# Moving the first mixer's causal convolution from VectorE to GpSimd

## The reference, cut to what matters

```
proj = x @ w_in                       # xm, zm, us: 512 channels each
xc = silu(causal_dwconv(xm, conv_w, conv_b))   # 4 taps per channel, plus bias
q, k = block-diagonal maps of xc;  v = block-diagonal map of xm
h = mlstm_chunkwise(q, k, v, gates of [q, k, v])
out_m = (headnorm(h) + skip * xc) * silu(zm)
y = gelu(s5_ssm(us, ...))             # a diagonal complex state space, 32 groups of 64 states
out_s = y * sigmoid(y @ w_glu + b_glu)
return concat(out_m, out_s) @ w_out
```

## Time and profile before

| | |
|---|---|
| time, median of 3 runs | 2026.87 us (2026.23 to 2027.75) |
| the profiled execution's own time | 2031.62 us |
| its span, first to last instruction | 2029.8 us |
| busy: PE, DVE, ACT, POOL | 1661.1, 736.8, 258.5, 94.4 us |
| mean granted clock of TensorE | 0.915 of full speed |
| the mixer's stage | about 1263 to 1375 us of the span |

### The profile page before, as it was taken

One profiled execution on the slowest core, in us unless ns is written; L12 is line 12 of the kernel. 1 busy time (PEld: TensorE's weight loads), 2 busy tenths in 40 slices (PEclk: granted clock), 3 DMA queues, 4 the chain that ended last, 5 costly groups with the idle time before them and its releaser, 6 DMA issues.

```text
span 2029.8 us, 25027 instructions
## 1 busy us (share of the span) xinstructions
PE 1661.1 (82%) x10024; PEld 996.5 (49%) x10025; DVE 736.8 (36%) x1491; ACT 258.5 (13%) x630; POOL 94.4 (5%) x125
## 2 busy tenths in 40 slices
PE   5999988866666578886757567989999999999998
PEld 3755553322222146332222124776997486769963
DVE  2764462211011127221101013974566323444672
ACT  1002120000000012000000002232111122311100
POOL 1001001000000000840000000000000000000000
PEclk9989999988787779998787888999999999999999
DMA  9989269999999995999999998204445273304351
GB/s 362 402 318 414 94 276 410 420 422 422 422 422 422 404 422 219 400 405 421 422 422 422 422 420 330 101 1 176 149 142 207 80 283 120 129 11 166 125 208 41
DMA packets 122677, 581.28 MB, mean 286 GB/s; under 512 B 10820, under 2 KB 15272, under 8 KB 67160
## 3 DMA queue, kind: packets, MB, share of 16 engines
q1 hardware_dynamic: 120416, 573.92, 70.6%
q0 software_dynamic: 1104, 2.86, 0.4%
q10 hardware_dynamic: 1064, 3.17, 0.4%
HBM read 578.88 MB, written 1.05 MB: 286 GB/s over the span
## 4 chain that ended last, share of the span: by engine, by line
PE 43%; DMA 33%; DVE 8%; PEld 8%; issue 4%; ACT 2%; SPq 1%; PEldq 1%; DVEq 0%; ACTq 0%
DMA ring_buffer<-in_exp_w 30%; PE ps L1472 7%; PE ps L2197 6%; PE ps L2168 6%; PEld ps L2168 5%; PE ps L1497 4%; PE ps L2886 4%; PE ps L1997 3%; DMA ring_buffer<-in_attn_w_in 1%; PE ps L997 1%; PE ps L2877 1%; SPq L1361 1%; PE ps L2139 1%; PEld ps L829 1%; DVE xn L537 1%
## 5 line engine op out<-in xcount | busy, mean ns | idle before, releaser
L1472 PE MATMUL ps<-ring_buffer,arena 128*32 128x512 f32 x1984 | 298.4, 760 | 174.6 <-DMA ring_buffer<-in_exp_w 171.7
L1472 PEld LDWEIGHTS ps<-ring_buffer,arena 128*32 128x32 f32 x1984 | 78.2, 135 | 381.1 <-issue 324.6
L1497 PE MATMUL ps<-ring_buffer,arena 128*32 128x512 f32 x1088 | 149.7, 701 | 87.3 <-DMA ring_buffer<-in_exp_w 75.4
L1668 DVE TENSOR_TENSOR arena<-arena,ps 128x512 f32<-128x512 f32 x18 | 19.2, 1064 | 412.5 <-PE ps L1472 412.5
L2168 PE MATMUL ps<-arena,ring_buffer 128*128 128x128 f32 x1152 | 133.9, 276 | 3.7 <-issue 3.7
L2168 PEld LDWEIGHTS ps<-arena,ring_buffer 128*128 128x128 f32 x1152 | 130.8, 192 | 5.7 <-issue 5.7
L1497 PEld LDWEIGHTS ps<-ring_buffer,arena 128*32 128x32 f32 x1088 | 40.1, 126 | 186.1 <-issue 145.5
L2197 PE MATMUL ps<-ring_buffer,arena 128*128 128x512 f32 x252 | 111.0, 594 | 3.4 <-issue 2.4
L2168 PE MATMUL ps<-hT,ring_buffer 128*128 128x128 f32 x864 | 99.4, 275 | 0.0
L2168 PEld LDWEIGHTS ps<-hT,ring_buffer 128*128 128x128 f32 x864 | 97.9, 192 | 0.0
L1686 DVE TENSOR_TENSOR arena<-ps,gates 128x512 f32<-128x512 f32 x16 | 11.1, 693 | 195.1 <-PE ps L1497 195.1
(11 more groups left out here) (570 smaller groups left out, 2096.6 us busy)
## 6 DMA issues: line engine op xcount, KB each, us to landing
ring_buffer<-in_exp_w SPq DMA_DIRECT2D x376, 1024.0 KB, 18.6
ring_buffer<-in_ffn_w SPq DMA_DIRECT2D x30, 2048.0 KB, 11.8
ring_buffer<-in_ada_w SPq DMA_DIRECT2D x24, 2048.0 KB, 17.5
ring_buffer<-in_c_w_in SPq DMA_DIRECT2D x8, 2048.0 KB, 13.0
ring_buffer<-in_attn_w_in SPq DMA_DIRECT2D x6, 2048.0 KB, 16.8
arena<-in_exp_w SPq DMA_DIRECT2D x6, 1024.0 KB, 8.1
ring_buffer<-in_ab_w_in SPq DMA_DIRECT2D x3, 2048.0 KB, 14.0
ring_buffer<-in_ffn_w SPq DMA_DIRECT2D x6, 1024.0 KB, 6.0
```

The costliest lines, as they stand in the source:

```text
L1472: ins = pe.matmul(ps[c, bank, :], tokens[:, 4 * phase + k, c], halves[j][:, k, :], start=(phase == 0 and k == 0), stop=(phase == 1 and k = ...
L1497: ins = pe.matmul(ps[c, bank, :], tokens[:, 2 * phase + k, c], halves[j][:, k, half * 512:(half + 1) * 512], start=(phase == 0 and k == 0) ...
```

## The change

The four tiles' convolution leaves DVE's list and becomes a POOL function of the same stage. `convolve` and its two loops go from `all_dve`, so that `take_y(0)` follows `turn_out(0)`, and `turned_in(1)` follows `turn_in(1, 3)`. POOL has no instruction in use here that multiplies and adds a tile in one, so each tap beyond the first becomes two: a product by the tap into a scratch tile (`shifted`, the first tile of `xcT`, which ACT writes only later), and a sum onto `conv`. That makes 7 instructions for a tile instead of 4, and 28 instead of 16. Each is chained by `v`. The silu waits for the new semaphore `convolved`. To make room for it, two semaphores of the state space's parameters, each raised once by DVE, become one that counts to two.

```
-            SPREAD, CONVOLVED = 1, 2
+            SPREAD = 1
+            convolved, shifted = sem("ab_convolved"), xcT[:, 0, :]
...
-                act.wait_ge(conv_step, CONVOLVED)
+                act.wait_ge(convolved, 1)
                 act.activation(xcT, conv, ACT.Silu).then_inc(conv_done, 1)
...
-                def convolve(n):
...
                 turn_out(0)
-                for n in range(2):
-                    convolve(n)
                 take_y(0)
                 for i in range(4):
                     turn_in(1, i)
-                for n in range(2, 4):
-                    convolve(n)
                 turned_in(1)
...
-            stage(all_pe, all_act, all_dve)
+            def all_pool(pool):
+
+                v = chain["pool"]
+                pool.wait_ge(conv_step, SPREAD)
+                for n in range(4):
+                    pool.wait_ge(tile_taken, XM + n + 1)
+                    v(pool.tensor_scalar(conv[:, n, :], xm[:, n, 0:S], col("ab_conv_w_2", n), col("ab_conv_b_2", n),
+                                         ALU.mult, ALU.add))
+                    for j in range(1, M_CONV):
+                        v(pool.tensor_scalar(shifted, xm[:, n, j:j + S], col("ab_conv_w_2", 4 * j + n), None, ALU.mult))
+                        ins = pool.tensor_tensor(conv[:, n, :], conv[:, n, :], shifted, ALU.add)
+                        if n == 3 and j == M_CONV - 1:
+                            ins.then_inc(convolved, 1)
+                        else:
+                            v(ins)
+
+            stage(all_pe, all_act, all_dve, all_pool)
```

## The result

The changed kernel took 2046.28 us in the median of 4 runs, against 2026.55 us before, so the medians differ by 19.7 us. The ratio taken over the single runs is 1.0088, 95% interval 1.0068 to 1.0108: 14 to 22 us slower. The forecast was 2044.4, range 2037 to 2049.

What follows compares the result with a forecast made beforehand. The chain of waits ran through DVE, but PE's own list decided. PE 17.0 us late, less its 1.05 us wait, gives 16.0; plus 1.5 for the clock, 17.5; 2026.87 + 17.5 = 2044.4 us, range 2037 to 2049.

Steps and rivals of the forecast that it cites:

- At best 1.05 us: At `outputs(1)`: of DVE's 8.0 us saved, only PE's wait of 1.05 us for `turn_out(1)` can turn into time.
- POOL alone 24.1 us: In the convolution: POOL's 28 instructions with their gaps need 24.1 us undisturbed, or 18.8 with the low end.
- The form as the cause of 0.927: In POOL's twelve tap products: a `tensor_scalar` with a column and no second operation takes 0.927 us, against 0.482 with two.
- Turns, 1.0 + 13.7 - 4.4 = 10.3 us for POOL: In the convolution: POOL waits 1.0 and 13.7 us behind DVE's two-tile instructions, of which 4.4 us is hidden.
- Which instructions take turns: Beside POOL's convolution: `turn_out`, `turned_in` and presumably scans alternate with POOL at the port; `turn_in` and `take_y` do not.
- the others run freely: Beside POOL's convolution: DVE instructions that don't read two SBUF tiles are not held by POOL's work.
- The end of the convolution, 34.4 us after POOL's start: POOL starts at 1283.6 and ends the convolution at 1318.0, so the q, k, v products start 17.0 us later.
- The clock, 1.5 us: At the q, k, v products: after PE's longer pause, some 3 us of work at half speed loses 1.5 us.
- The rival with POOL keeping up: In the convolution: no turns and quick instructions, 1.1 to 2.6 us slower, 2029.4 us at most; chance 0.04.
- quick instructions with turns: In the convolution: all sixteen `tensor_scalar` at 0.482 us, with turns, 12.2 us slower in place of 17.5; chance 0.28.
- no turns: In the convolution: slow instructions but no turns with DVE, 7.2 us slower, 2034.1 us; chance 0.07.
- The rival in which scans take no turns: In the convolution: scans don't hold POOL, 15.1 us slower in place of 17.5, 2042.0 us; inside the forecast's range.

Runs made afterwards that it cites:

- experiment 1: The changed kernel with the convolution cut to its first tap, 4 POOL instructions in place of 28: ratio 1.0005 to the kernel before, mixer 111.02 us.
- experiment 5: The kernel with tiles 0 and 1 convolved by POOL with two-operation tap products, tiles 2 and 3 by DVE as before: ratio 0.9992 to the kernel before.
- experiment 2: The changed kernel with a second operation, times 1.0, in POOL's twelve tap products: ratio 1.0061 to the kernel before, mixer 124.01 us.
- experiment 4: The changed kernel with 70 unread products on PE before it waits for the convolution: ratio 1.0114 to the kernel before, mixer 138.34 us.
- experiment 3: The changed kernel without DVE's two-tile sums, scans and output rotation of chunk 1: ratio 1.0050 to the kernel before, mixer 123.43 us.
- experiment 7: The changed kernel with 37 unread products on PE before it waits for the convolution: ratio 1.0068 to the kernel before, mixer 127.14 us.
- experiment 6: The kernel before, convolution still on DVE, plus POOL's 28 instructions on a scratch tile nobody reads: ratio 1.0036 to the kernel before, mixer 120.15 us.

## Why the prediction was right

The direction, the size and the place were right; the terms of its sum, one by one:

- *At best 1.05 us:* the bound held; experiment 1 kept nothing, experiment 5 0.56 us. The reason, that behind this wait PE's own list decides and DVE waits for PE, was only half right. Up to `outputs(2)` DVE's list for chunk 2 was as long as PE's, and PE waited for it once more (0.42 us at 1331.88, in the kernel before). From `outputs(1)` to `outputs(2)` it took 24.2 us in the kernel before and in experiments 2, 4 and 5, though the gates took from 5.53 to 6.87 us in them. Since DVE's list for chunk 2 also starts from `outputs(1)`, the bound stayed what it was.
- *POOL alone 24.1 us:* 24.5 by experiment 3. The first `tensor_scalar` takes 0.55, not 0.482.
- *The form as the cause of 0.927:* shown by experiment 2. The Trainium skill (GPSIMD Engine Reference, Engine selection) calls one-input work roughly line-rate; here that describes the form with two operations (0.477, where VectorE's L2675 took 0.41), not the one with a single operation (0.925).
- *Turns, 1.0 + 13.7 - 4.4 = 10.3 us for POOL:* 9.0. The sum came out near, the picture behind it did not. I had POOL and DVE alternate strictly, which would have held DVE in chunk 1 by about 9 us. DVE's chunk 1 from L2652 to L2668 took 1303.62 - 1288.90 = 14.7 us, against 11.9 before, so it lost 2.8. The sums L2652 and L2653 were not stretched at all, and no scan by more than 0.5. The sign that I named for them, each stretched by about one POOL instruction, was wrong. It cost the forecast nothing, since DVE waited for PE afterwards in either case.
- *Which instructions take turns:* as forecast, `turn_in` kept its 1.22 us (1286.52) and POOL's tap beside it its 0.93 (1287.30). But "the others run freely" is too wide, as rows of the kernel before show (below).
- *The end of the convolution, 34.4 us after POOL's start:* 33.5. The q, k, v products were 54.70 - 38.46 = 16.2 us late, forecast 17.0.
- *The clock, 1.5 us:* 1.65 by experiment 7. It varies: in experiments 2 and 3, after pauses of 13.4 and 11.3 us, the same products lost 2.1 and 2.65.
- *What the sum lacked:* about 1 us later in the mixer. `outputs(1)` started 16.8 us late, where 16.0 + 1.5 was forecast, and `outputs(2)` 17.7. Between them PE did the gates and the first `zm` tile 1.6 us faster than before (5.84 and 5.07 us), gave that back in a wait of 1.44 us for DVE's L2686, and then needed 5.39 us for a `zm` tile (1338.48) that took 3.70 before; the clock was down again there.

These rows of the kernel before are the ones that "the others run freely" leaves out:

```profile
317.66 0.16 DVE L1661 TENSOR_SCALAR arena<-arena 128x4 f32<-128x4 f32 x1
...
828.36 0.73 POOL L481 TENSOR_TENSOR arena<-arena,hT 128x256 f32<-128x256 f32 x1
828.47 0.65 DVE L1661 TENSOR_SCALAR arena<-arena 128x4 f32<-128x4 f32 x1
```

L1661, a `tensor_scalar` with a single SBUF tile, took 0.16 us where POOL was idle and 0.65 beside POOL's L481, and ended 0.03 us after it. (What lay beside L484 in that trace was a comparison of two SBUF tiles, L1637, not a sum.)

The errors in the terms that counted are small, 1.3 us at most, and of both signs: 17.5 forecast, 17.7 in the mixer, 0.0088 x 2026.55 = 17.8 by the ratio of the runs, and 19.7 by their medians. That the sum came within 0.2 us of the mixer's 17.7 is luck, because the convolution's end was set 0.9 us too late, about as much as was missing later; that the size came out is not.

The rival with POOL keeping up failed on both its conditions, the low price and the free port. With the low price alone (experiment 2) the mixer was still 13.1 us longer, near the 12.2 that the forecast gave for quick instructions with turns. With the port nearly free (experiment 3) it was 12.5, more than the 7.2 given for no turns, since the turns at the start remained and PE's clock cost more. The rival in which scans take no turns fails on the scans of up to 1.15 us and on POOL's sums of 1.11 beside them.

## What to carry to other kernels

Before moving work to an idle engine, ask how early its result must be there, and which wait the freed engine ends: here 8 us off VectorE could end one wait of 1.05 us, while the result had 1.2 us to spare. GpSimd's price for a small elementwise step depends on its form, so look for a row of just that form. And GpSimd beside VectorE's instructions of two SBUF tiles costs both sides; find stretches where VectorE reads PSUM or waits, and give GpSimd no more than fits there.

## What the runs showed of the hardware that I had not expected

- A GpSimd `tensor_scalar` of 128x256 float32 with one operation takes 0.925 us, with a second, idle one 0.477, and with a multiply and an add by two columns 0.55.
- Sharing is not even. A GpSimd tap queued beside two back-to-back VectorE instructions on SBUF tiles waited through both (2.81 and 2.84 us, 1.76 when they were chained), and those two were hardly delayed.
- Scans share more mildly than whole instructions would: beside GpSimd's work one took 0.66 to 1.15 us where it takes 0.66, and GpSimd's sums took 1.11 where they take 0.725. The Trainium skill (SBUF — State Buffer, Who interferes with whom) calls the shared ports an exclusive lock; for whole instructions as the profile records them the scans don't bear that out. The tap at 1293.27 and the scan at 1293.64 ended within 0.1 us of each other, and each lost only about 0.25 us. Which part of an instruction holds the port was not tried.
- In nine of the ten profiled executions, the kernel before among them, the granted clock of TensorE fell with PE busy, within the gates' 48 small products or right behind them. The gates and the `zm` tile behind them took 10.9, 12.6 or 14.2 us together in these nine, and 16.5 in experiment 6. So a microsecond won or lost ahead of such a stretch can vanish in it; what decides between these times no run shows.
